# Expert outputs added onto the residual rows in DRAM by indirect DMA, and a last stage of load, norm and store

## The chip, the core and the metric

The kernel runs on one core of a Trainium2 chip. The metric is the device time of one execution in microseconds, as the median of several; less is better.

## What is computed

One decoder block on 2048 tokens of 1024 features, float32. A mixer (gated DeltaNet heads beside dilated window attention) gives the residual rows x2. Then a mixture of experts follows, which the change touches: 32 experts, two for each token, each a SwiGLU with 256 hidden features. At the end stands an RMSNorm of the sum.

```python
xs = xt[buf_tok].reshape(nblk, MOE_BLK, d)
def expert_block(args):
    xb, e = args
    hid = jax.nn.silu(xb @ w_gate[e]) * (xb @ w_up[e])
    return hid @ w_down[e]
ys = lax.map(expert_block, (xs, blk_e)).reshape(P, d)
out = jnp.zeros((T, d), ys.dtype).at[buf_tok].add(ys * buf_w[:, None])
# x = x2 + gate * out ; result = rmsnorm(x, norm_final)
```

`buf_w` is the router's weight of a token for an expert, and `gate` a vector over features that is the same for all tokens.

## The kernel before

Eight stages run one after the other, with a barrier of all engines between them (`PHASES`, L2164). Tensors keep 128 rows on the partitions; the 2048 tokens are 16 tiles.

`mix_out` (L1463) makes the residual rows tile by tile, keeps them in SBUF (`m.x2`, L2210) and stores the normed rows `h` to `m.h_d` (L1657, on ScalarE's queue). Its `residual` on ScalarE (L1652) takes the squares of a tile and then waits for `h`.

`route` (L1684) picks two experts for each token. The tokens of an expert fill whole blocks of 128 slots, up to 96 blocks; here 50 are in use. `m.dest` holds the slot of each token and choice. Thirty-two small indirect DMAs of GpSimd scatter the token numbers into `slot_tok_d` (L1870), which is loaded back as `m.slot_tok`. Unused slots hold token 0.

`experts` (L1876) goes over the blocks in use, with buffers for two blocks (b = 0, 1) and for two experts' weights. Each engine has its own program, in order:

- SP loads the weights of the expert after next: `wgu` (2 MB, L1923) when `gu_done` says that the last block before has been multiplied with it, `wd` (1 MB, L1925) when `y_done` does. The two counters come from the router (`by_expert`). At the end it writes zeros into the unused blocks of `ys_d` (L1935).
- GpSimd gathers the 128 rows of a block from `h_d` (L1949), as soon as the block two earlier has been transposed and the indices are there (L1945 to L1948).
- TensorE, in step t: `turn_x` transposes block t+1 (L1959), `down` makes the output of block t-1 (L1986), then it transposes the hidden tile of t (L2004), and `gate_up` of t+1 follows (L1976).
- ScalarE, in step t: `silu` (L2026), the copy of the transposed rows of t+1 (L2016), the copy of the transposed hidden tile (L2032), and the store of block t-1's output into its own place in `ys_d` (L2020).
- VectorE, in step t: the hidden product (L2058), the indices of block t+2 (L2050), and `take_y` of t-1, the output times `gate` (L2047).

`finish` (L2067) takes the tiles in groups of four. GpSimd gathers the two expert rows of each token from `ys_d` (two indirect DMAs a tile, L2103), ScalarE scales one by its router weight (L2113), VectorE scales and adds the other and adds x2 from SBUF (L2141, L2142), ScalarE takes squares and root (L2116, L2117), VectorE norms (L2146), and ScalarE issues the store (L2120).

A signal's `n(k)` is the semaphore value after k events; `credit` is a start value that every wait adds too.

Of the kernel before, what the change touches and what calls it, by code (L numbers as in the profile page):

```python
# [11 lines left out]
P = 128  # L12
T = 2048
# [1449 lines left out]
def mix_out(nc, m, a):  # L1463
# [5 lines left out]
    with Room(nc, "mo") as R:  # L1469
# [23 lines left out]
        h_out = S("h_out", 2, 16)  # L1493
# [7 lines left out]
        with R.block() as block:  # L1501
# [124 lines left out]
            def _(act):  # L1626
# [54 lines left out]
                for b in range(2):  # L1681
                    act.wait_ge(*h_out[b].n(NT // 2))
                    act.wait_ge(*lg_ready[b].n(NT // 2))
def route(nc, m, a):  # L1684
# [8 lines left out]
    with Room(nc, "ro") as R:  # L1693
# [28 lines left out]
        toki = R.sb("toki", [P, NT], I32)  # L1722
        zero = R.sb("zero", [P, NBLK], I32)
# [15 lines left out]
        with R.block() as block:  # L1739
            @block.sync  # L1740
            def _(sp):

                sp.wait_ge(*zero_set.n(1))
                sp.dma_start(m.slot_tok_d, zero[:, :]).then_inc(*zero_out.inc)
                sp.wait_ge(*tok_all.n(1))
                sp.dma_start(m.slot_tok[:, 0:NBLK], m.slot_tok_d).then_inc(*tok_in.inc)
                sp.wait_ge(*tok_in.n(1))

            @block.vector
            def _(dve):  # L1750
# [11 lines left out]
                V.memset(zero[:, :], 0).then_inc(*zero_set.inc)  # L1762
                link(V.memset(m.slot_tok[:, NBLK:NBLK + 1], 0))
# [46 lines left out]
                link(V.tensor_copy(toki[:, :], m.cst[:, C_TOK:C_TOK + NT]))  # L1810
# [53 lines left out]
            def _(pool):  # L1864
                pool.wait_ge(*pos_ready.n(1))
                pool.wait_ge(*zero_out.n(1))
                flat = m.slot_tok_d.rearrange("p b -> (p b)").unsqueeze(1)
                for t in range(NT):
                    for n in range(2):
                        pool.indirect_dma_start(out=flat, out_offset=bass.IndirectOffsetOnAxis(ap=pos[:, n, t:t + 1].bitcast(U32), axis=0),  # L1870
                                                in_=toki[:, t:t + 1], in_offset=None).then_inc(tok_out, 16)
# [4 lines left out]
def experts(nc, m, a):  # L1876
# [4 lines left out]
    with Room(nc, "ex") as R:  # L1881
        idx = R.sb("idx", [P, 2], I32)
# [12 lines left out]
        zero_set, zero_out, seen_sp = R.sig("zero_set"), R.sig("zero_out", 16), R.plain("seen_sp")  # L1895
        seen_act = R.plain("seen_act")
# [3 lines left out]
        ht_done, ht_ready, y_ready, out = S("ht_done"), S("ht_ready"), S("y_ready"), S("out", 2, 16)  # L1900
# [13 lines left out]
        with R.block() as block:  # L1914
            @block.sync
            def _(sp):
                with sp.Fori(0, NE // 2) as i:
# [12 lines left out]
                pairs = sp.value_load(m.pairs[0:1, 0:1], min_val=1, max_val=NBLK // 2 - 1)  # L1930
                sp.wait_ge(*zero_set.n(1))
                with sp.Fori(0, NBLK // 2 - 1) as i:
                    with sp.If(pairs <= i):
                        for b in range(2):
                            sp.dma_start(one(m.ys_d, 2 * i + (2 + b)), zero[:, :]).then_inc(*zero_out.inc)  # L1935
                unused = sp.value_load(m.pairs[0:1, 1:2], min_val=0, max_val=NBLK // 2 - 1)
                sp.wait_ge(*zero_out.n(unused * 2))
                sp.sem_inc(seen_sp, 1)

            @block.gpsimd  # L1940
            def _(pool):
                rows = m.h_d.rearrange("t p n -> (t p) n")
                for t, b, q, head, tail in blocks(pool):

                    pool.wait_ge(*xt_done[b].n(q))  # L1945
# [4 lines left out]
                                            in_offset=bass.IndirectOffsetOnAxis(ap=idx[:, b:b + 1].bitcast(U32), axis=0)).then_inc(xg_in[b], 16)  # L1950

# [59 lines left out]
            def _(act):  # L2011
# [6 lines left out]
                def store_y(t, b, q):  # L2018
                    act.wait_ge(*y_ready[b].n(q + 1))
                    act.dma_start(one(m.ys_d, t), y[:, b, :]).then_inc(*out[b].inc)  # L2020

                take_x(0, 0, 0)
                for t, b, q, head, tail in blocks(act):
# [12 lines left out]
                for b in range(2):  # L2036
                    act.wait_ge(*out[b].n(q + 1))
                    act.sem_inc(seen_act, 1)

            @block.vector  # L2040
            def _(dve):
                nc.vector.memset(zero[:, :], 0.0).then_inc(*zero_set.inc)

                def take_y(t, b, q):
                    dve.wait_ge(*y_done.n(t + 1))
                    dve.wait_ge(*out[b].n(q))
                    nc.vector.tensor_tensor(y[:, b, :], ps[:, 6:8, :].rearrange("p n w -> p (n w)"), gate, ALU.mult).then_inc(*y_ready[b].inc)  # L2047
# [19 lines left out]
def finish(nc, m, a):  # L2067
# [3 lines left out]
    with Room(nc, "fi") as R:  # L2071
        idx = R.sb("idx", [P, NBUF, 2], I32)
        yg = R.sb("yg", [P, NBUF, 2, D])
# [3 lines left out]
        ss = R.sb("ss", [P, NBUF])  # L2077
        eps = R.sb("eps", [P, 1])
        def S(name, step=1):
            return R.sigs(name, NBUF, step)  # L2080

        gain_in, eps_set = R.sig("gain_in", 16), R.sig("eps_set")
        yg_in, seen = [R.plain(f"yg_in{b}") for b in range(NBUF)], R.plain("seen")
        idx_ready, scaled, sum_ready, sq_ready, o_ready, out = S("idx_ready"), S("scaled"), S("sum_ready"), S("sq_ready"), S("o_ready"), S("out", 16)
        dve_self, act_self = R.plain("dve_self"), R.plain("act_self")
        N = NT // NBUF
        with R.block() as block:
            @block.sync
            def _(sp):
                sp.dma_start(gain[:, :], row_bc(a["norm_final"], D)).then_inc(*gain_in.inc)  # L2090

            @block.gpsimd
            def _(pool):
                rows = m.ys_d.rearrange("t p n -> (t p) n")
                with pool.Fori(0, N) as i:
                    for b in range(NBUF):

                        pool.wait_ge(*sum_ready[b].n(i))
                        pool.sem_inc(seen, 1)
                        pool.wait_ge(*idx_ready[b].n(i + 1))  # L2100
                        pool.sem_inc(seen, 1)
                        for n in range(2):
                            pool.indirect_dma_start(out=yg[:, b, n, :], out_offset=None, in_=rows,  # L2103
                                                    in_offset=bass.IndirectOffsetOnAxis(ap=idx[:, b, n:n + 1].bitcast(U32), axis=0)).then_inc(yg_in[b], 16)

            @block.scalar
            def _(act):
                link = Chain(act, act_self)
                act.wait_ge(*eps_set.n(1))
                with link.loop(N, NBUF) as i:  # L2110
                    for b in range(NBUF):
                        act.wait_ge(yg_in[b], i * 32 + 32)
                        nc.scalar.activation(yg[:, b, 0, :], yg[:, b, 0, :], ACT.Copy, scale=m.gate[:, 0, bass.ds(NBUF * i + b, 1)]).then_inc(*scaled[b].inc)  # L2113
                    for b in range(NBUF):
                        act.wait_ge(*sum_ready[b].n(i + 1))
                        link(nc.scalar.activation(junk[:, :], o[:, b, :], ACT.Square, accum_out=ss[:, b:b + 1]))  # L2116
                        nc.scalar.activation(ss[:, b:b + 1], ss[:, b:b + 1], ACT.Sqrt, bias=eps[:, :], scale=1.0 / D).then_inc(*sq_ready[b].inc)  # L2117
                    for b in range(NBUF):
                        act.wait_ge(*o_ready[b].n(i + 1))
                        act.dma_start(one(m.out, NBUF * i + b), o[:, b, :]).then_inc(*out[b].inc)  # L2120
                for b in range(NBUF):
                    act.wait_ge(*out[b].n(N))

            @block.vector
            def _(dve):
                link = Chain(dve, dve_self)
                V = nc.vector
                V.memset(eps[:, :], EPS).then_inc(*eps_set.inc)
                dve.wait_ge(*gain_in.n(1))

                def take_idx(t, b):
                    V.tensor_copy(idx[:, b, :], m.dest[:, :, bass.ds(t, 1)].rearrange("p n a -> p (n a)")).then_inc(*idx_ready[b].inc)  # L2132

                def tiles(i, ahead):
                    for b in range(NBUF):
                        dve.wait_ge(*scaled[b].n(i + 1))
                        dve.wait_ge(yg_in[b], i * 32 + 32)
                        if ahead:
                            take_idx(NBUF * i + NBUF + b, b)
                        dve.wait_ge(*out[b].n(i))  # L2140
                        link(V.scalar_tensor_tensor(o[:, b, :], yg[:, b, 1, :], m.gate[:, 1, bass.ds(NBUF * i + b, 1)], yg[:, b, 0, :], ALU.mult, ALU.add))  # L2141
                        V.tensor_tensor(o[:, b, :], o[:, b, :], one_tile(m.x2, NBUF * i + b), ALU.add).then_inc(*sum_ready[b].inc)  # L2142
                    for b in range(NBUF):
                        dve.wait_ge(*sq_ready[b].n(i + 1))
                        link(V.reciprocal(ss[:, b:b + 1], ss[:, b:b + 1]))  # L2145
# [114 lines left out]
```

## Time and profile before

| | us |
|---|---|
| median of 3 runs | 2682.29 |
| lowest and highest | 2680.24, 2687.91 |
| the profiled execution, its own time | 2681.78 |
| its span in the trace | 2679.9 |

| engine | busy us | share |
|---|---|---|
| TensorE, matmul | 2272.5 | 85% |
| VectorE | 1104.7 | 41% |
| ScalarE | 805.8 | 30% |
| GpSimd | 329.6 | 12% |

The span goes from the first instruction to the last. PE is TensorE, DVE VectorE, ACT ScalarE, POOL GpSimd, SP SyncE; a q behind the name is that engine's sequencer, which issues DMAs. The DMA line of the page gives the busy share of the 16 DMA engines in tenths, for 40 equal slices of the span, each 67 us. "Landing" is the time from the issue of a DMA to its last arrival.

### The profile page before, as it was taken

To read this page: it belongs to the slowest core of one execution; us is meant where nothing else is said; L and a number is where in the kernel's file an instruction comes from. 1 tells how busy PE (TensorE), PEld (TensorE's weight loads), DVE (VectorE), ACT (ScalarE), POOL (GpSimd) and SP (SyncE) were. 2 spreads that over 40 slices of the span, in tenths; PEclk is the share of its full clock that TensorE was granted. 3 is DMA by queue.
4 is the path that set the end of the run, shared out by engine and by line. 5 is a ranking of instruction groups with operands and counts; after the bars stand their busy time and mean duration, and the time that the engine had idled before them with its cause. 6 is when DMAs were issued, how large, how long until landed. Compare 5 with 4: busy or idle time off the path is not lost. (4 is left out here: it accounts for less than half of the span.)

```text
span 2679.9 us, 31777 instructions
## 1 busy us (share of the span) xinstructions
PE 2272.5 (85%) x9218; PEld 1329.4 (50%) x9219; DVE 1104.7 (41%) x2029; ACT 805.8 (30%) x2123; POOL 329.6 (12%) x314
## 2 busy tenths in 40 slices
PE   3999899999888978949999959999169999999940
PEld 2666444444444458926777735555024444444410
DVE  5444132322346525526788845654501111111127
ACT  1433111111333112216777834442011111111125
POOL 0000000000111014411133400000310000000022
PEclk9999999999999989969999979999579999999975
DMA  8443011112456549723233333331058766579767
GB/s 337 146 135 135 33 55 63 55 63 87 137 176 194 176 130 296 237 97 115 95 88 95 104 110 127 127 127 44 5 186 308 242 229 218 202 265 328 270 249 283
DMA packets 178532, 426.63 MB, mean 159 GB/s; under 512 B 41824, under 2 KB 77920, under 8 KB 162960
## 3 DMA queue, kind: packets, MB, share of 16 engines
q1 hardware_dynamic: 153664, 335.37, 36.9%
q0 software_dynamic: 12832, 43.02, 4.7%
q10 hardware_dynamic: 11952, 47.19, 4.3%
q8 instruction: 45, 0.74, 0.1%
q14 instruction: 39, 0.32, 0.0%
HBM read 304.44 MB, written 121.07 MB: 159 GB/s over the span
## 5 line engine op out<-in xcount | busy, mean ns | idle before, releaser
L627 PE MATMUL ps<-big,pc_w 128*128 128x512 f32 x1280 | 556.8, 596 | 10.1 <-DMA pc_w<-in_w_chan 10.1
L627 PEld LDWEIGHTS ps<-big,pc_w 128*128 128x128 f32 x1280 | 243.3, 191 | 310.5 <-issue 299.5
L1976 PE MATMUL ps<-ex_wgu,ex_xt 128*128 x800 | 359.1, 602 | 24.2 <-DMA ex_wgu<-in_w_gate_up 23.5
L1976 PEld LDWEIGHTS ps<-ex_wgu,ex_xt 128*128 128x128 f32 x800 | 150.3, 193 | 198.9 <-issue 198.9
L310 PE MATMUL ps<-cp_wt,big 128*128 128x344 f32 x768 | 225.5, 454 | 0.0
L1562 PE MATMUL ps<-w_out,mo_yt 128*128 128x512 f32 x512 | 225.0, 598 | 0.0
L1372 PE MATMUL ps<-at_v,at_pt 128*128 128x128 f32 (+1 forms) x1200 | 183.1, 290 | 6.2 <-DMA at_v<-v_d 6.2
L1986 PE MATMUL ps<-ex_wd,ex_hidt 128*128 x400 | 181.8, 598 | 4.3 <-issue 2.9
L310 PEld LDWEIGHTS ps<-cp_wt,big 128*128 128x128 f32 x768 | 145.9, 191 | 76.9 <-issue 4.1
L1434 ACT ACTIVATE at_p<-at_p,at_low 128x256 f32<-128x256 f32 (+1 forms) x384 | 174.0, 456 | 20.1 <-DVE at_low L1401 19.7
L1372 PEld LDWEIGHTS ps<-at_v,at_pt 128*128 128x128 f32 x1200 | 149.1, 191 | 52.8 <-issue 35.7
L2058 DVE TENSOR_TENSOR ex_hid<-ex_sg,ps 128x256 f32<-128x256 f32 x50 | 21.1, 421 | 362.1 <-ACT ex_sg L2026 340.1
L1562 PEld LDWEIGHTS ps<-w_out,mo_yt 128*128 128x128 f32 x512 | 97.2, 192 | 116.5 <-issue 116.5
L1399 DVE SCALAR_TENSOR_TENSOR at_p<-ps,bias 128x512 f32<-128x512 f32 (+1 forms) x192 | 109.3, 569 | 69.9 <-PE ps L1347 69.4
L2047 DVE TENSOR_TENSOR ex_y<-ps,mod 128x1024 f32<-128x1024 f32 x50 | 61.2, 1225 | 174.6 <-PE ps L1986 174.6
L2026 ACT ACTIVATE ex_sg<-ps 128x256 f32<-128x256 f32 x50 | 19.3, 386 | 356.7 <-PE ps L1976 356.7
L1347 PE MATMUL ps<-at_kb,at_qb 64*128 64x256 f32 (+1 forms) x768 | 119.5, 389 | 6.1 <-POOL at_kb L1333 5.1
L1949 POOL DMA_INDIRECT ex_xg<-h_d,ex_idx x50 | 47.3, 945 | 545.9 <-DVE ex_idx L2050 499.2
L1417 ACT COPY at_pt<-ps 128x512 f32<-128x512 f32 (+1 forms) x192 | 93.8, 488 | 66.5 <-PE ps L1357 61.1
L782 DVE TENSOR_SCALAR pc_cv<-pc_pre,pc_wc 128x2048 f32<-128x2048 f32 x12 | 15.4, 1287 | 234.5 <-ACT pc_pre L707 234.5
L1401 DVE TENSOR_REDUCE at_low<-at_p 128x2 f32<-128x512 f32 (+1 forms) x192 | 109.4, 570 | 6.6
L1986 PEld LDWEIGHTS ps<-ex_wd,ex_hidt 128*128 128x128 f32 x400 | 72.7, 192 | 78.2 <-issue 78.2
(289 smaller groups left out, 2866.5 us busy)
## 6 DMA issues: line engine op xcount, KB each, us to landing
ex_wgu<-in_w_gate_up SPq DMA_DIRECT2D x32, 2048.0 KB, 11.1
ex_wd<-in_w_down SPq DMA_DIRECT2D x32, 1024.0 KB, 7.8
ys_d<-ex_y ACTq DMA_DIRECT2D x50, 512.0 KB, 8.0
cp_w<-in_w_ada SPq DMA_DIRECT2D x24, 1024.0 KB, 5.4
ch_d<-pc_cv SPq DMA_DIRECT2D x20, 1024.0 KB, 3.9
at_v<-v_d SPq DMA_DIRECT2D x27, 512.0 KB, 3.9
o_d<-at_o SPq DMA_DIRECT2D x48, 264.0 KB, 2.1
mo_o<-o_d SPq DMA_DIRECT2D x16, 792.0 KB, 6.6
```

The source lines that it names most:

```text
L310: last = nc.tensor.matmul(ps[:, ROW_A + g, 0:THIRD], m.ht[:, k, t * P:(t + 1) * P], wt[:, k, g * THIRD:(g + 1) * THIRD], start=(k == 0), s ...
L627: last = nc.tensor.matmul(ps[:, n % 2, :], w[:, ch % 2, k, :], m.ht[:, k, g * BANK:(g + 1) * BANK], start=(k == 0), stop=(k == KD - 1))
L1347: last = nc.tensor.matmul(ps[:, 2 * (s % 2) + h, lo:2 * P], qb[r, b, s, :], kb[r, b, s, lo:], start=True, stop=True)
L1372: last = nc.tensor.matmul(ps[:, 6 + b, w], pt[:, e, h, k, :], v[:, b, k, w], start=(k == k0), stop=(k == 1))
L1399: nc.vector.scalar_tensor_tensor(p[:, s, :, lo:], ps[:, 2 * e:2 * e + 2, lo:2 * P], DH ** -0.5, m.bias[:, unit[0][1], 2 * s:2 * s + 2, lo: ...
L1401: nc.vector.tensor_reduce(low[:, b, 2 * s:2 * s + 2], p[:, s, :, lo:], AX.X, ALU.max, negate=True).then_inc(*max_ready[e].inc)
L1417: nc.scalar.copy(pt[:, e, :, k:, :], ps[:, 4 + e, :].rearrange("p (h k n) -> p h k n", h=2, k=2)[:, :, k:, :]).then_inc(*pt_ready[e].inc)
L1434: ins = nc.scalar.activation(p[:, s, h, lo:], p[:, s, h, lo:], ACT.Exp, bias=low[:, b, at:at + 1], accum_out=low[:, b, at + AH:at + AH + 1])
L1562: last = nc.tensor.matmul(ps[:, 2 + 2 * b + n, :], yt[:, b, k, :], w[:, k, n * BANK:(n + 1) * BANK], start=(k == 0), stop=(k == KD - 1))
L1976: last = nc.tensor.matmul(ps[:, 2 + b, :], xt[:, b, k, :], wgu[:, bass.ds(half * WGU + k * 2 * DE, 2 * DE)], start=(k == 0), stop=(k == KD ...
L1986: last = nc.tensor.matmul(ps[:, 6 + n, :], hidt[:, b, k, :], wd[:, bass.ds(half * WD + (k * D + n * BANK), BANK)], start=(k == 0), stop=(k ...
L2047: nc.vector.tensor_tensor(y[:, b, :], ps[:, 6:8, :].rearrange("p n w -> p (n w)"), gate, ALU.mult).then_inc(*y_ready[b].inc)
```

## The change

- `mix_out` also stores each tile of x2 to a new DRAM tensor `acc_d`, on ScalarE's queue, before it waits for `h`.
- `route` scatters pairs of the token number and its router weight (8 bytes in place of 4). Unused slots now hold the numbers T to T+127, which are an extra tile of `h_d` and of `acc_d`, and the weight 0.
- `experts` writes zeros into those two extra tiles first, and GpSimd waits for them. `take_y` multiplies by the slot's router weight and by `gate` in one instruction, and copies the row numbers into `to`. GpSimd adds the block's rows onto `acc_d` with an accumulating indirect DMA, one block after the other: each add waits until ScalarE has seen the one before land. ScalarE issues no store. The zeros into unused blocks go.
- `finish` loads a tile of `acc_d` (SP), takes squares and root (ScalarE), norms (VectorE) and stores (SP). There are no gathers, no scaling and no sums in it.

```diff
@@ mix_out, ScalarE, residual
+                    act.dma_start(one(m.acc_d, t), x2(b, q)).then_inc(*x2_out.inc)
                     act.wait_ge(*h_ready[b].n(q + 1))
@@ route
+                for n in range(2):
+                    link(V.tensor_copy(toki[:, n, :, 0], m.cst[:, C_TOK:C_TOK + NT]))
+                    link(V.tensor_copy(toki[:, n, :, 1].bitcast(F32), m.gate[:, n, :]))
@@ experts
+        added = R.sig("added", credit=2)
@@ experts, SP
+                sp.wait_ge(*zero_set.n(1))
+                sp.dma_start(m.h_d[NT], zero[:, :]).then_inc(*zero_out.inc)
+                sp.dma_start(m.acc_d[NT], zero[:, :]).then_inc(*zero_out.inc)
@@ experts, GpSimd
-                for t, b, q, head, tail in blocks(pool):
-
+                sums = m.acc_d.rearrange("t p n -> (t p) n")
+
+                def gather(b, q):
                     pool.wait_ge(*xt_done[b].n(q))
                     pool.sem_inc(seen, 1)
                     pool.wait_ge(*idx_ready[b].n(q + 1))
                     pool.sem_inc(seen, 1)
                     pool.indirect_dma_start(out=xg[:, b, :], out_offset=None, in_=rows,
                                             in_offset=bass.IndirectOffsetOnAxis(ap=idx[:, b:b + 1].bitcast(U32), axis=0)).then_inc(xg_in[b], 16)
+
+                def add_y(s, b, q):
+
+                    pool.wait_ge(*y_ready[b].n(q + 1))
+                    pool.sem_inc(seen, 1)
+                    pool.wait_ge(*added.n(s))
+                    pool.sem_inc(seen, 1)
+                    pool.indirect_dma_start(out=sums, out_offset=bass.IndirectOffsetOnAxis(ap=to[:, b:b + 1].bitcast(U32), axis=0),
+                                            in_=y[:, b, :], in_offset=None, compute_op=ALU.add).then_inc(out[b], 16)
+
+                pool.wait_ge(*zero_out.n(2))
+                gather(0, 0)
+                for t, b, q, head, tail in blocks(pool):
+                    if not tail:
+                        gather(*after(b, q))
+                    if not head:
+                        add_y(t - 1, *before(b, q))
+                add_y(t, 1, q)
@@ experts, ScalarE
                     if not head:
-                        store_y(t - 1, *before(b, q))
-                store_y(t, 1, q)
+                        b1, q1 = before(b, q)
+                        act.wait_ge(out[b1], q1 * 16 + 16)
+                        act.sem_inc(*added.inc)
+                act.wait_ge(out[1], q * 16 + 16)
+                act.sem_inc(*added.inc)
@@ experts, VectorE, take_y
-                    dve.wait_ge(*out[b].n(q))
-                    nc.vector.tensor_tensor(y[:, b, :], ps[:, 6:8, :].rearrange("p n w -> p (n w)"), gate, ALU.mult).then_inc(*y_ready[b].inc)
+                    dve.wait_ge(*added.n(t - 1))
+                    nc.vector.tensor_copy(to[:, b:b + 1], m.slot_tok[:, bass.ds(t, 1), 0])
+                    nc.vector.scalar_tensor_tensor(y[:, b, :], ps[:, 6:8, :].rearrange("p n w -> p (n w)"), m.slot_tok[:, bass.ds(t, 1), 1].bitcast(F32), gate, ALU.mult, ALU.mult).then_inc(*y_ready[b].inc)
@@ finish
+                def load(t):
+                    if t >= NBUF:
+                        sp.wait_ge(*o_ready.n(t - NBUF + 1))
+                    sp.dma_start(x[:, t % NBUF, :], m.acc_d[t]).then_inc(*x_in[t % NBUF].inc)
...
+                for t in range(NT):
+                    sp.wait_ge(*o_ready.n(t + 1))
+                    sp.dma_start(m.out[t], o[:, t % NBUF, :]).then_inc(*out[t % NBUF].inc)
+                    if t + NBUF < NT:
+                        load(t + NBUF)
```

## Rows read from the trace of the kernel before

**Rows 1.** The page: DMA engines' busy share in tenths, 40 slices of the span
```profile
DMA  8443011112456549723233333331058766579767
```

**Rows 2.** TensorE's waits, 1990 to 2582 us: waiter, releaser, total us, times, longest
```profile
PE ps L1976 <- DMA ex_wgu<-in_w_gate_up: 19.3, 12, 2.9
...
PE ps L1959 <- DMA ex_xg<-h_d,ex_idx: 1.8, 2, 1.5
```

**Rows 3.** Timeline of one block: start us, us, engine, line, operation, tiles, count
```profile
2082.66 1.22 DVE L2047 TENSOR_TENSOR ex_y<-ps,mod 128x1024 f32<-128x1024 f32 x1 [3.41 <-PE ps L1986]
2082.68 7.03 PE L1976 MATMUL ps<-ex_wgu,ex_xt 128*128 x16
...
2089.55 1.04 PE L1959 MATMUL ps<-cst,ex_xg 128*128 128x128 f32 x8
...
2090.67 0.14 DVE L2050 COPY ex_idx<-slot_tok 128x1 int32 x1
...
2091.62 0.94 POOL L1949 DMA_INDIRECT ex_xg<-h_d,ex_idx  x1 [10.62 <-DVE ex_idx L2050]
...
2094.06 1.23 DVE L2047 TENSOR_TENSOR ex_y<-ps,mod 128x1024 f32<-128x1024 f32 x1 [3.24 <-PE ps L1986]
```

**Rows 4.** Tiles ex_xg, ex_y, ex_wd: count, ns min/median/max, first and last start; landing
```profile
L1949 POOL DMA_INDIRECT ex_xg<-h_d,ex_idx x50: 943/944/977, 1959.5 to 2545.0; - x50
...
DMA to landing us min/median/max: 4.2/5.0/10.9
...
L2047 DVE TENSOR_TENSOR ex_y<-ps,mod x50: 1223/1225/1226, 1993.7 to 2579.5; 128x1024 f32<-128x1024 f32 x50
...
L1925 SPq DMA_DIRECT2D ex_wd<-in_w_down x32: 332/333/343, 1961.4 to 2524.8; - x32
...
DMA to landing us min/median/max: 5.4/7.8/16.4
```

**Rows 5.** Timeline of SP's queue, 2060 to 2085 us: weight loads as issued
```profile
2060.00 0.33 SPq L1925 DMA_DIRECT2D ex_wd<-in_w_down  x1
2067.09 0.33 SPq L1923 DMA_DIRECT2D ex_wgu<-in_w_gate_up  x1
2082.80 0.33 SPq L1925 DMA_DIRECT2D ex_wd<-in_w_down  x1
2084.99 0.34 SPq L1923 DMA_DIRECT2D ex_wgu<-in_w_gate_up  x1
```

**Rows 6.** Windows: us, busy (x) PE PEld DVE ACT POOL; then PEclk, DMA share, GB/s
```profile
2010.00:2015.00 5.00, 5.00 (x19) 2.60 (x18) 0.48 (x2) 1.40 (x2) 0.90 (x1) 1.00 1.04 427
...
2020.00:2030.00 10.00, 10.00 (x27) 4.78 (x26) 0.48 (x2) 1.17 (x2) 0.00 (x0) 0.83 0.80 320
...
2450.00:2500.00 50.00, 44.76 (x132) 21.20 (x130) 6.37 (x12) 7.08 (x12) 3.78 (x4) 1.00 0.88 323
...
2600.00:2680.00 80.00, 0.00 (x0) 0.00 (x0) 62.03 (x76) 47.32 (x70) 25.85 (x25) 0.50 0.77 286
```

**Rows 7.** Timeline of the first block of the expert stage
```profile
1970.26 9.88 PE L1976 MATMUL ps<-ex_wgu,ex_xt 128*128 x16 [4.20 <-DMA ex_wgu<-in_w_gate_up]
```

**Rows 8.** Timeline of the last stage: its first DMA, first copy and last instruction
```profile
2586.05 0.36 SPq L2090 DMA_DIRECT2D fi_gain<-in_norm_final  x1
2589.77 0.38 DVE L2132 COPY fi_idx<-dest 128x2 int32<-128x2 int32 x4 [4.73 <-DMA fi_gain<-in_norm_final]
...
2674.66 1.29 DVE L2146 SCALAR_TENSOR_TENSOR fi_o<-fi_o,fi_ss,fi_gain 128x1024 f32<-128x1024 f32 x1
```

**Rows 9.** Tile fi_o of the last stage: scaled sums and squares
```profile
L2141 DVE SCALAR_TENSOR_TENSOR fi_o<-fi_yg,gate x16: 1276/1278/1286, 2600.3 to 2667.8; 128x1024 f32<-128x1024 f32 x16
...
L2116 ACT ACTIVATE fi_junk<-fi_o x16: 1039/1040/1057, 2607.3 to 2670.4; 128x1024 f32<-128x1024 f32 x16
```

**Rows 10.** Groups of the mixer's output stage, ScalarE: busy, mean ns, idle before, releaser
```profile
L1633 ACT ACT_TABLE_LOAD x13 | 16.7, 1283 | 44.4 <-DVE mo_h L1608 44.4
```

**Rows 11.** Tile ro_toki of the route stage: the scatters
```profile
L1870 POOL DMA_INDIRECT slot_tok_d<-ro_toki,ro_pos x32: 963/967/2230, 1910.5 to 1951.8; - x32
```

More of the change, by code:

```diff
@@ L1492, in mix_out @@
         x2_ready, xsq_ready, h_ready = S("x2_ready"), S("xsq_ready"), S("h_ready")
-        h_out = S("h_out", 2, 16)
+        h_out, x2_out = S("h_out", 2, 16), R.sig("x2_out", 16)
         def x2(b, q):
@@ L1682, in _ @@
                     act.wait_ge(*h_out[b].n(NT // 2))
+                    act.wait_ge(*x2_out.n(NT))
                     act.wait_ge(*lg_ready[b].n(NT // 2))
@@ L1721, in route @@
         sq2 = R.sb("sq2", [P, NE, NE])
-        toki = R.sb("toki", [P, NT], I32)
-        zero = R.sb("zero", [P, NBLK], I32)
+        toki = R.sb("toki", [P, 2, NT, 2], I32)
+        blank = R.sb("blank", [P, NBLK, 2], I32)
         ps = m.ps
@@ L1760, in first_of @@
                     link(V.tensor_tensor(one_hot, iota(n), over(idx[:, :], n), ALU.is_equal))
-                V.memset(zero[:, :], 0).then_inc(*zero_set.inc)
-                link(V.memset(m.slot_tok[:, NBLK:NBLK + 1], 0))
+                link(V.tensor_scalar(blank[:, :, 0], m.cst[:, C_TOK:C_TOK + 1].to_broadcast([P, NBLK]), float(T), None, ALU.add))
+                V.memset(blank[:, :, 1], 0).then_inc(*zero_set.inc)
+                dve.wait_ge(*zero_set.n(1))
+                link(V.tensor_copy(m.slot_tok[:, NBLK, :], blank[:, 0, :]))
                 link(V.tensor_reduce(gm[:, :], gl, AX.X, ALU.max))
@@ L1866, in _ @@
                 pool.wait_ge(*zero_out.n(1))
-                flat = m.slot_tok_d.rearrange("p b -> (p b)").unsqueeze(1)
+                flat = m.slot_tok_d.rearrange("p b x -> (p b) x")
                 for t in range(NT):
@@ L1881, in experts @@
     with Room(nc, "ex") as R:
-        idx = R.sb("idx", [P, 2], I32)
+        idx, to = R.sb("idx", [P, 2], I32), R.sb("to", [P, 2], I32)
+        by = R.sb("by", [P, 2])
         xg = R.sb("xg", [P, 2, D])
@@ L1899, in experts @@
         xt_done, xt_ready, sg_ready, hid_ready = S("xt_done"), S("xt_ready"), S("sg_ready"), S("hid_ready")
-        ht_done, ht_ready, y_ready, out = S("ht_done"), S("ht_ready"), S("y_ready"), S("out", 2, 16)
+        ht_done, ht_ready, y_ready, out = S("ht_done"), S("ht_ready"), S("y_ready"), [R.plain("out0"), R.plain("out1")]
+        added = R.sig("added", credit=2)
         gate = m.mod[:, 5 * D:6 * D]
@@ L1928, in _ @@
                     sp.wait_ge(*wd_in[b].n(NE // 2))
[L1930 to L1938, printed above, removed]
             @block.gpsimd
@@ L2016, in take_x @@
                     nc.scalar.copy(xt[:, b, :, :].rearrange("p k n -> p (k n)"), ps[:, 0:2, :].rearrange("p k n -> p (k n)")).then_inc(*xt_ready[b].inc)
-                def store_y(t, b, q):
-                    act.wait_ge(*y_ready[b].n(q + 1))
-                    act.dma_start(one(m.ys_d, t), y[:, b, :]).then_inc(*out[b].inc)
                 take_x(0, 0, 0)
@@ L2033, in _ @@
                     if not head:
-                        store_y(t - 1, *before(b, q))
-                store_y(t, 1, q)
-                for b in range(2):
-                    act.wait_ge(*out[b].n(q + 1))
-                    act.sem_inc(seen_act, 1)
+                        b1, q1 = before(b, q)
[3 more added lines that the diff above has]
+                act.sem_inc(*added.inc)
             @block.vector
@@ L2071, in finish @@
     with Room(nc, "fi") as R:
-        idx = R.sb("idx", [P, NBUF, 2], I32)
-        yg = R.sb("yg", [P, NBUF, 2, D])
+        x = R.sb("x", [P, NBUF, D])
         gain = R.sb("gain", [P, D])
@@ L2076, in finish @@
         junk = R.sb("junk", [P, D])
-        ss = R.sb("ss", [P, NBUF])
+        ss = R.sb("ss", [P, NT])
         eps = R.sb("eps", [P, 1])
-        def S(name, step=1):
-            return R.sigs(name, NBUF, step)
         gain_in, eps_set = R.sig("gain_in", 16), R.sig("eps_set")
-        yg_in, seen = [R.plain(f"yg_in{b}") for b in range(NBUF)], R.plain("seen")
-        idx_ready, scaled, sum_ready, sq_ready, o_ready, out = S("idx_ready"), S("scaled"), S("sum_ready"), S("sq_ready"), S("o_ready"), S("out", 16)
+        x_in, out = R.sigs("x_in", NBUF, 16), R.sigs("out", NBUF, 16)
+        sq_ready, o_ready = R.sig("sq_ready"), R.sig("o_ready")
         dve_self, act_self = R.plain("dve_self"), R.plain("act_self")
-        N = NT // NBUF
         with R.block() as block:
@@ L2089, in _ @@
             def _(sp):
-                sp.dma_start(gain[:, :], row_bc(a["norm_final"], D)).then_inc(*gain_in.inc)
[L2092 to L2104, printed above, removed]
+                def load(t):
+                    if t >= NBUF:
+                        sp.wait_ge(*o_ready.n(t - NBUF + 1))
+                    sp.dma_start(x[:, t % NBUF, :], m.acc_d[t]).then_inc(*x_in[t % NBUF].inc)
+                load(0)
+                load(1)
+                sp.dma_start(gain[:, :], row_bc(a["norm_final"], D)).then_inc(*gain_in.inc)
+                for t in range(2, NBUF):
+                    load(t)
+                for t in range(NT):
[3 more added lines that the diff above has]
+                        load(t + NBUF)
+                for b in range(NBUF):
+                    sp.wait_ge(*out[b].n(NT // NBUF))
             @block.scalar
@@ L2109, in _ @@
                 act.wait_ge(*eps_set.n(1))
[L2110 to L2122, printed above, removed]
+                for t in range(NT):
+                    b = t % NBUF
+                    act.wait_ge(*x_in[b].n(t // NBUF + 1))
+                    link(nc.scalar.activation(junk[:, :], x[:, b, :], ACT.Square, accum_out=ss[:, t:t + 1]))
+                    nc.scalar.activation(ss[:, t:t + 1], ss[:, t:t + 1], ACT.Sqrt, bias=eps[:, :], scale=1.0 / D).then_inc(*sq_ready.inc)
             @block.vector
@@ L2126, in _ @@
                 link = Chain(dve, dve_self)
-                V = nc.vector
-                V.memset(eps[:, :], EPS).then_inc(*eps_set.inc)
+                nc.vector.memset(eps[:, :], EPS).then_inc(*eps_set.inc)
                 dve.wait_ge(*gain_in.n(1))
[L2131 to L2145, printed above, removed]
-                        V.scalar_tensor_tensor(o[:, b, :], o[:, b, :], ss[:, b:b + 1], gain[:, :], ALU.mult, ALU.mult).then_inc(*o_ready[b].inc)
-                for b in range(NBUF):
-                    take_idx(b, b)
-                with link.loop(N - 1, 2 * NBUF) as i:
-                    tiles(i, True)
-                tiles(N - 1, False)
+                for t in range(NT):
+                    b = t % NBUF
+                    dve.wait_ge(*sq_ready.n(t + 1))
+                    link(nc.vector.reciprocal(ss[:, t:t + 1], ss[:, t:t + 1]))
+                    dve.wait_ge(*x_in[b].n(t // NBUF + 1))
+                    dve.wait_ge(*out[b].n(t // NBUF))
+                    nc.vector.scalar_tensor_tensor(o[:, b, :], x[:, b, :], ss[:, t:t + 1], gain[:, :], ALU.mult, ALU.mult).then_inc(*o_ready.inc)
 class Shared:
@@ L2199, in block_kernel @@
         m.o_d = dram("o_d", [NB, NT, P, AW + 2 * AH])
-        m.h_d = dram("h_d", [NT, P, D])
-        m.slot_tok_d = dram("slot_tok_d", [P, NBLK], I32)
-        m.ys_d = dram("ys_d", [NBLK, P, D])
+        m.h_d, m.acc_d = dram("h_d", [NT + 1, P, D]), dram("acc_d", [NT + 1, P, D])
+        m.slot_tok_d = dram("slot_tok_d", [P, NBLK, 2], I32)
         m.ch_d = dram("ch_d", [m.NCH, P, T])
```

14 lines of the change are left out of this document (6 added, 8 removed).

## The prediction

> **What bounds the kernel now.** I read the page's slices first. In the last quarter the DMA digits stand at 5 to 9 [rows 1]: the expert stage, where 3 MB of weights per expert stream past TensorE. The wait list of TensorE for that stage is nearly empty: 19.3 us in 12 waits for `ex_wgu`, 1.8 us for gathered rows [rows 2]. So TensorE bounds the stage, with DMA close behind. The timeline of one block gives the cycle [rows 3]. Call T the moment at which VectorE takes block t-1's output (2082.66). Then `gate_up` of t+1 runs 7.03 us, the transposes of `turn_x` for t+2 start at T+6.9, `down` of t follows, and its output is taken at 2094.06. That is a block of 11.4 us, of which 4.5 us lie between the start of `turn_x` and the next T. Over the stage 49 blocks take from 1993.7 to 2579.5, mean 11.95 [rows 4]. The rest over 11.4 is mostly weights that come late.
>
> What matters is when the gather for t+2 starts. Today GpSimd issues it 0.8 us after the index copy, which is before T: in these rows the copy is at 2090.67, the gather at 2091.62 and the T of that round at 2094.06, so 2.4 us before T [rows 3]. It has some 9.4 us until `turn_x`, and lands in 4.2 us at best, 5.0 in the median, 10.9 at worst [rows 4]. All of that is hidden.
>
> **The change, part by part.**
>
> *Expert stage, GpSimd's order.* This is the term that decides. GpSimd's program becomes: gather(t+1), add(t-1), gather(t+2), add(t), and so on, and each add waits for `y_ready`. GpSimd works in order, so gather(t+2) stands behind the wait of add(t-1). Step by step from T: VectorE copies the row indices (0.14, as the index copy) and runs the scaled product, priced at 1.28 as its kind costs in the last stage [rows 9], so `y_ready` is at T+1.4. GpSimd reacts after 0.8 [rows 3], so the add starts at T+2.2. An indirect DMA holds GpSimd 0.94 us [rows 4], and with the gap the 32 scatters of the route stage come every 1.33 us [rows 11], so gather(t+2) is issued at T+3.5. It must have landed by T+6.9: 3.4 us, where the shortest of 50 gathers took 4.2. TensorE must wait in every block, even if the add itself is free: T+7.7.
>
> *What the add adds.* No row shows an accumulating transfer. From below it is one copy of 512 KB, 1.2 us at the 427 GB/s that the DMA engines reached in one stretch [rows 6], and since it is issued 1.3 us ahead it then delays the gather by nothing. From above nothing in the trace limits it. I take two copies' time, 2.5 us, because it reads the product and the old row and writes one: the gather lands 1.2 us later, at T+8.9. For the high end I take four copies, 4.9 us, T+11.4. The Trainium skill (Collectives: The Full Stack, "The bandwidth ceiling") says that a reduce in the DMA engines runs at about half the rate of a copy because it reads two sources; no run here shows it, and it would leave the sum as it is.
>
> A block without other load is then 8.9 + 4.5 = 13.4 us.
>
> *Blocks under weight load.* SP issues `wd` of a coming expert 0.14 us after T, and in 19 of the 30 cases `wgu` follows 1.9 to 2.2 us later (in the others 7 us or more) [rows 5]. There 1 MB and 2 MB (2.5 and 4.9 us) stand before or beside the add (2.5) and the gather (1.2) on the same engines. The fixed part of a transfer is 2.9 to 3.0 us: 4.2 less 1.2 for the gather, 5.4 less 2.5 for `wd` [rows 4]. The gather, last in its queue, lands at 0.14 + 2.9 + 2.5 + 4.9 + 2.5 + 1.2 = T+14.1, so such a block is 18.6 us. Today some of these blocks are late already: they hold the 19.3 us of waits for `ex_wgu` [rows 2], and the DMA engines move 323 GB/s over 50 us [rows 6].
>
> Stage: 19 x 18.6 + 30 x 13.4 = 755 us against 586 now: **+170**.
>
> *TensorE's clock.* In one stretch of 10 us TensorE was granted 0.83 of its full clock, so 1.2 GHz for part of it, right after it had stood waiting, and the first `gate_up` after a long pause took 9.88 us instead of 7.03 [rows 6, 7]. In the 19 loaded blocks TensorE would idle 7 us before `turn_x`, and the work after it lies in the loop. I take 1.5 us each, half of that 2.85: **+28**; from below nothing, from above 1.5 us in all 49, +73.
>
> *ScalarE's new wait.* It no longer issues the store but waits until the add has landed before it takes `silu` of t+1. Behind it are `sg`, `hid` and then `turn_x`'s copy. The add always lands before the gather that is queued behind it, and `sg` and `hid` (under 1 us) fit into the 4.5 us after that gather. Cost nothing, as long as the gather is the later one. The wait of each add for the one before is covered too: the add lands some 5.5 us after its issue, 11 under load, and the next is due a block later.
>
> *The product on VectorE* costs 1.28 instead of 1.22: counted in T+1.4.
>
> *Last stage.* From its first DMA at 2586 to the end of the span at 2680 it now takes 94 us; the last instruction starts at 2674.66 [rows 8]. It moves 25 MB (32 gathers and 16 stores of 512 KB); the new one moves 16.8 MB (16 loads, 16 stores). At 427 GB/s that is 39 us, at the stage's 286 [rows 6] it is 59; I take 350, 48 us. ScalarE (1.04 for the square, some 0.5 for the rest) and VectorE (1.29 plus a reciprocal) need some 1.5 us a tile [rows 8, 9], less than the 3 us of DMA, and four buffers hold it: a load of 3.7 us (as the gain's, 2586.05 to 2589.77), the two engines and the issues make 8 us for four tiles. First landing at 2589.8 and last tile plus store add about 8: 56 us. **-38** (-48 to -27).
>
> *Entry.* The weights are issued behind two stores of zeros (1 MB, 2.5 us), and the first gather, issued at 1959.5 so far [rows 4], waits for both to land, some 4 us. The first `gate_up` at 1970.26 waits for weights [rows 7]: **+3** (0 to 6). *Exit:* instead of two stores the last two adds, one after the other, each 0.8 us later through GpSimd and with 1.2 us more of data: **+5** with the landing between them (2 to 10). The zeros into unused blocks stood behind the last weight load, beside TensorE's work, and free nothing on the path.
>
> *Mixer and route.* 16 more stores of 512 KB on ScalarE's queue, 0.33 us to issue each, as SP's loads [rows 4]: ScalarE has 44.4 us of idle time right behind that place [rows 10], and DMA is a third busy there [rows 1]. If that cover went, 5 us. The scatters carry 8 bytes instead of 4; GpSimd's pitch sets them. Three more small copies: **+1**.
>
> **Sum:** 170 + 28 - 38 + 3 + 5 + 1 = +169 on the profiled execution's 2681.8 us (span 2679.9), 0.5 us under the median of 2682.3: **2850 us**. Low end: gather at T+7.7 in quiet blocks (12.2) and 16.0 in loaded ones gives +84, no clock loss, the last stage at -48: about 2723. High end: the add at four copies gives 15.9 and 21.1, +292, the clock +73, the last stage -27, +12 at the ends: about 3030.
>
> **Rivals.** (1) *The gather hides after all: faster.* It needs the gather to land within 3.4 us of its issue, with the add not in its way. Then only the last stage and the ends count, 2682 - 38 + 8 = 2652. Against it: 4.2 is the least of 50 [rows 4]. For it: an unloaded transfer of this size could in principle be near that edge, and GpSimd could react quicker. The Trainium skill (DMA: Bandwidth & Descriptors, "Anatomy of one DMA") fits a GpSimd DMA as 2.0 us plus bytes over 436 GB/s; that makes 3.2 us for this gather and would give this very case; the trace disagrees, with 4.2 at least. Chance 0.06. The point from which it decides: at less than 0.7 us of wait a block the last stage pays for it all.
> (2) *The add is slow and everything follows its landing.* Each block is then 2.2 + D + 1.2 + 4.5, D the add's time to landing. D = 15 gives 22.9 us a block, +536, about 3190 with the rest. Nothing in the trace speaks for or against it but the rate of a copy. Chance 0.13.
> (3) *Gains and stalls cancel:* the same, between 2674 and 2690, chance 0.02. The forecast with its bounds has 0.79.
>
> **Numbers.** The chance of faster by over 0.3% (about what a measurement of this kernel tells from no change) is rival 1, 0.06; within 0.3% 0.02; slower 0.92. The range 2735 to 3010 leaves out rivals 1 to 3 for the most part and the thin ends of the bounds.
>
> **What the profile after would show.** TensorE's wait for `ex_xg` before `turn_x` rises from 1.8 us to 100 to 250 us, with 45 or more waits, and its wait for `ex_wgu` shrinks. The gather starts about 3.5 us after VectorE begins `ex_y`, right behind the add on GpSimd, and lands 5 to 11 us later. ScalarE's `sg` waits for a DMA instead of TensorE. The last stage ends some 56 us after its start. The forecast is wrong if TensorE's wait is small (the gather was quicker), if the add's landing takes over 12 us, or if the wait of `turn_x` is for ScalarE or GpSimd and not for the gather.

## The result, and the profile after

The changed kernel takes 2986.11 us (median of 4 runs, 2982.82 to 2995.98) against 2682.22: a ratio of 1.1135, 95% interval 1.1104 to 1.1167. That is 304 us slower. The forecast was 2850, with a range of 2735 to 3010: the time lies inside the range, 24 us under its upper end, and the forecast itself was 136 us short.

The spans of the two profiled executions, cut at the first and last product `ex_y` and at the first DMA of the last stage, say where the time went:

| stretch, us | before | after | difference | forecast |
|---|---|---|---|---|
| up to the first `ex_y` | 1993.7 | 2002.1 | +8.4 | +4 |
| first to last `ex_y`, 49 blocks | 585.8 | 915.6 | +329.8 | +198 |
| last `ex_y` to the last stage's first DMA | 6.5 | 15.1 | +8.6 | +5 |
| last stage, to the end of the span | 93.9 | 48.2 | -45.7 | -38 |
| span | 2679.9 | 2981.0 | +301.1 | +169 |

TensorE's waits in the expert stage, 1990 to 2918 us, which answer to [rows 2] (waiter, releaser, total us, times, longest):

```profile
PE ps L1978 <- DMA ex_xg<-h_d,ex_idx: 265.1, 47, 9.1
```

It was 1.8 us in 2 waits, and is now 265.1 in 47, at the line of `turn_x`. No wait for weights is left. The timeline of one quiet block, that is one without a load of `wgu` right behind T, to be read against [rows 3]:

```profile
2258.63 7.03 PE L1995 MATMUL ps<-ex_wgu,ex_xt 128*128 x16
2258.72 0.15 DVE L2062 COPY ex_to<-slot_tok 128x1 int32 x1 [13.59 <-PE ps L2005]
...
2258.85 1.28 DVE L2063 SCALAR_TENSOR_TENSOR ex_y<-ps,slot_tok,mod 128x1024 f32<-128x1024 f32 x1
2261.14 1.59 POOL L1959 DMA_INDIRECT acc_d<-ex_y,ex_to  x1 [20.57 <-DVE ex_y L2063]
2263.04 0.97 POOL L1950 DMA_INDIRECT ex_xg<-h_d,ex_idx  x1 [0.30 <-issue]
2268.28 0.38 ACT L2041 ACTIVATE ex_sg<-ps 128x256 f32<-128x256 f32 x1 [9.07 <-DMA acc_d<-ex_y,ex_to]
...
2269.57 1.09 PE L1978 MATMUL ps<-cst,ex_xg 128*128 128x128 f32 x8 [3.91 <-DMA ex_xg<-h_d,ex_idx]
2270.50 5.30 PE L2005 MATMUL ps<-ex_wd,ex_hidt 128*128 x8
...
2276.03 0.15 DVE L2062 COPY ex_to<-slot_tok 128x1 int32 x1 [6.77 <-PE ps L2005]
```

T, at which VectorE turns to block t-1's output, is 2258.72. GpSimd's lines show the two indirect DMAs back to back, the add at T+2.4 and the gather behind it at T+4.3. TensorE has finished `gate_up` at 2265.66 and stands 3.91 us. Then `down`, 3.60 us before, takes 5.30. The block is 17.3 us where it was 11.4. Of the 49 blocks 27 are quiet like this one (15.0 to 18.1 us, median 16.9), 20 take 20.3 to 23.4, and the last two are short.

The tiles `ex_xg` and `ex_y` of the same kernel (count, ns min/median/max, first and last start; below each the time to landing), for [rows 4]:

```profile
L1950 POOL DMA_INDIRECT ex_xg<-h_d,ex_idx x50: 938/975/978, 1965.3 to 2885.6; - x50
...
DMA to landing us min/median/max: 5.6/6.7/13.2
...
L2063 DVE SCALAR_TENSOR_TENSOR ex_y<-ps,slot_tok,mod x50: 1283/1284/1285, 2002.1 to 2917.7; 128x1024 f32<-128x1024 f32 x50
L1959 POOL DMA_INDIRECT acc_d<-ex_y,ex_to x50: 1549/1592/1634, 2004.4 to 2920.4; - x50
...
DMA to landing us min/median/max: 6.0/6.4/12.1
```

An accumulating indirect DMA holds GpSimd for 1.59 us, where a gather holds it for 0.98, and lands after 6.4 us in the median. ScalarE is idle for 501.4 us in front of `silu` until adds have landed, which looks like a cause. It was a rival in the experiments.

The windows show the clock (columns as in [rows 6]):

```profile
2250.00:2300.00 50.00, 40.60 (x102) 19.46 (x102) 5.21 (x10) 4.92 (x8) 7.70 (x6) 0.86 0.41 111
2700.00:2800.00 100.00, 59.84 (x154) 30.30 (x153) 8.08 (x18) 7.70 (x14) 11.76 (x10) 0.81 0.61 202
```

TensorE's granted clock is 0.86 and 0.81 on average, so part of nearly every block runs at 1.2 GHz. It was 1.00 over the 50 us from 2450 before [rows 6]. The DMA engines move 111 and 202 GB/s, less than the 323 before, so on average they are not the bound; within a loaded block the gather still waits behind the weights, as the experiments show.

The page's group of `down`, first before and then after, says what the clock costs there:

```profile
L1986 PE MATMUL ps<-ex_wd,ex_hidt 128*128 x400 | 181.8, 598 | 4.3 <-issue 2.9
...
L2005 PE MATMUL ps<-ex_wd,ex_hidt 128*128 x400 | 237.6, 750 | 4.1 <-issue 4.1
```

The same 400 matmuls take 56 us more. Over the stage (1994 to 2580 us before, 2002 to 2918 after) TensorE is busy 559 us before and 645 after, for the same matmuls: 86 of the 330 us are what half clock costs, and the other 244 are waiting.

### The profile page after: what moved, and what is told of

It is laid out like the page before. It is cut to its first block and busy times, and to the rows that moved or that the text cites. A ratio compares the mean times of both kernels' runs of the same rounds, so it can differ in the third digit from the quotient of the medians.

```text
span 2981.0 us, 31595 instructions
## 1 busy us (share of the span) xinstructions
PE 2360.1 (79%) x9218; PEld 1375.4 (46%) x9219; DVE 1075.2 (36%) x2035; ACT 779.4 (26%) x2100; POOL 377.2 (13%) x332
## 5 line engine op out<-in xcount | busy, mean ns | idle before, releaser
L1978 PE MATMUL ps<-cst,ex_xg 128*128 128x128 f32 x400 | 84.5, 381 | 339.6 <-DMA ex_xg<-h_d,ex_idx 339.6
L1978 PEld LDWEIGHTS ps<-cst,ex_xg 128*128 128x128 f32 x400 | 66.4, 195 | 381.0 <-DMA ex_xg<-h_d,ex_idx 233.8
L2005 PE MATMUL ps<-ex_wd,ex_hidt 128*128 x400 | 237.6, 750 | 4.1 <-issue 4.1
L1959 POOL DMA_INDIRECT acc_d<-ex_y,ex_to x50 | 79.6, 1592 | 791.3 <-DVE ex_y L2063 402.6
L2041 ACT ACTIVATE ex_sg<-ps 128x256 f32<-128x256 f32 x50 | 19.2, 383 | 529.0 <-DMA acc_d<-ex_y,ex_to 501.4
L2005 PEld LDWEIGHTS ps<-ex_wd,ex_hidt 128*128 128x128 f32 x400 | 98.1, 259 | 112.4 <-issue 112.4
L2062 DVE COPY ex_to<-slot_tok 128x1 int32 x50 | 7.7, 154 | 336.5 <-PE ps L2005 336.5
```

The source lines that it names most:

```text
L1959: pool.indirect_dma_start(out=sums, out_offset=bass.IndirectOffsetOnAxis(ap=to[:, b:b + 1].bitcast(U32), axis=0), in_=y[:, b, :], in_offse ...
L1978: last = nc.tensor.transpose(ps[:, k // 4, (k % 4) * P:(k % 4 + 1) * P], xg[:, b, k * P:(k + 1) * P], m.ident)
L2005: last = nc.tensor.matmul(ps[:, 6 + n, :], hidt[:, b, k, :], wd[:, bass.ds(half * WD + (k * D + n * BANK), BANK)], start=(k == 0), stop=(k ...
```

## The experiments

The theory: gather(t+2) stands behind the wait and the issue of add(t-1) in GpSimd's program, and TensorE waits for it. The rivals: the accumulating transfer itself, and ScalarE's wait for its landing. Ratios are against the kernel before, run on the same chip (2677.26 us for the first four runs, 2681.10 for the last three, 2682.22 for the change itself), so a difference of two medians from different groups can be off by some 5 us. Each run's expert stage is its first to last `ex_y`.

### The gather first

```diff
                 gather(0, 0)
+                gather(1, 0)
                 for t, b, q, head, tail in blocks(pool):
                     if not tail:
-                        gather(*after(b, q))
+                        gather(b, q + 1)
                     if not head:
                         add_y(t - 1, *before(b, q))
                 add_y(t, 1, q)
+                pool.wait_ge(xg_in[0], q * 16 + 32)
```

It gathers one block more than is used.

> The changed kernel, GpSimd issuing the gather of block t+2 before the add of block t-1. Theory (the gather stands behind the wait and issue of the add, and TensorE waits for it): the gather is early again, TensorE's wait for ex_xg before turn_x falls from some 400 us to under 40, quiet blocks go from 16.9 us back to 11.4, blocks under weight load to 12 to 14.5, limited by ScalarE's wait for the landing. Whole kernel 2660 us, 2640 to 2710. Rival A (the add itself is slow, or ScalarE's wait for it sets the pace): the order hardly matters, over 2900.

Measured: 2707.56 us, ratio 1.0115 (1.0078 to 1.0153); the stage takes 641.1 us, 275 less than with the add first. The wait for `ex_xg` is gone. What TensorE waits for now, in the stage's wait lists of TensorE and of all engines:

```profile
PE ps L2025 <- DVE ex_hid L2076: 47.4, 15, 5.2
```

```profile
ACT ex_sg L2043 <- DMA acc_d<-ex_y,ex_to: 464.3, 44, 15.0
...
PEld ps L2025 <- DVE ex_hid L2076: 63.0, 20, 6.0
```

It waits for the hidden tile in 20 blocks. In 15 of them its matmul waits too, 47.4 us in all. The 63.0 us of the weight loads cover the same waits, so the two must not be added (the 110 us in the expectation of `both` are such a sum). The hidden tile waits for `silu`, which waits for the landing of the add. So putting the gather first takes away five sixths of the stage's loss, and behind it the rival's wait appears as the next bound. The time is 48 us over the value I had named, though inside its range.

### ScalarE does not wait

The order stays that of the change; GpSimd itself waits for the add before and then raises `added`, for VectorE. (The loop is peeled by two blocks, so that no wait has the value zero.)

```diff
-                    pool.wait_ge(*added.n(s))
-                    pool.sem_inc(seen, 1)
+                    if not is_tile(s, 0):
+                        b1, q1 = before(b, q)
+                        pool.wait_ge(out[b1], q1 * 16 + 16)
+                        pool.sem_inc(*added.inc)
...
-                    if not head:
-                        b1, q1 = before(b, q)
-                        act.wait_ge(out[b1], q1 * 16 + 16)
-                        act.sem_inc(*added.inc)
```

> The changed kernel with its order kept, but ScalarE no longer waits for the landing of an add; GpSimd waits for it itself before the next add. Theory (the gather's place is the cause, ScalarE's wait lies under it): the same time within 15 us of 2986. Rival A (ScalarE's wait in front of silu, 501 us of idle time in the profile, sets the pace): falls by over 150 us.

Measured: 2987.32 us, 1.1147 (1.1094 to 1.1199), stage 914.6 against 915.6. The 501 us of ScalarE's waiting cost nothing in this order. In the profile after, `silu` could start 0.8 us or more before `turn_x` in every block (1.3 us in the one shown), and TensorE needs the hidden tile only behind `turn_x` and `down`. The rival is out as the cause of the loss.

### No accumulate

```diff
-                                            in_=y[:, b, :], in_offset=None, compute_op=ALU.add).then_inc(out[b], 16)
+                                            in_=y[:, b, :], in_offset=None).then_inc(out[b], 16)
```

The rows are written over and not added, so this kernel leaves the sums out.

> The changed kernel with the accumulate left out of the indirect DMA: the rows are written instead of added, so the sums are left out of the computation. Theory: GpSimd needs 0.95 instead of 1.59 us to issue it and the transfer takes one copy's time instead of two, so the gather behind it lands 1.8 us earlier: 49 x 1.8 = 90 us less, 2895, 2860 to 2930; blocks still 14.5 us and more, since the order is kept. Rival B (accumulating is the cost, not the order): back to some 2700.

Measured: 2846.66 us, 1.0630 (1.0595 to 1.0664), stage 785.6, so rival B is out: with the accumulate gone and the order kept, 200 of the stage's 330 us stay. Its tile `ex_y`:

```profile
L1959 POOL DMA_INDIRECT acc_d<-ex_y,ex_to x50: 962/986/997, 1997.7 to 2783.2; - x50
...
DMA to landing us min/median/max: 3.3/3.8/11.1
```

So the accumulate costs 0.6 us more on GpSimd (1.59 against 0.99), and 2.7 us more from issue to landing at best (6.0 against 3.3), of which 2.1 lie behind GpSimd's part. The fall of 139 us is larger than expected, and the time is 13 us under my range. A quiet block shows why:

```profile
2241.50 0.15 DVE L2062 COPY ex_to<-slot_tok 128x1 int32 x1 [7.37 <-PE ps L2005]
...
2245.22 0.96 POOL L1950 DMA_INDIRECT ex_xg<-h_d,ex_idx  x1 [0.30 <-issue]
...
2249.82 1.09 PE L1978 MATMUL ps<-cst,ex_xg 128*128 128x128 f32 x8 [1.38 <-DMA ex_xg<-h_d,ex_idx]
2250.75 3.60 PE L2005 MATMUL ps<-ex_wd,ex_hidt 128*128 x8
...
2254.59 0.15 DVE L2062 COPY ex_to<-slot_tok 128x1 int32 x1 [5.03 <-PE ps L2005]
```

TensorE waits only 1.38 us, and `down` is at 3.60 us again: full clock. The block is 13.1 us. With the accumulate it waits 3.9 us and pays 1.7 us more at half clock (6.5 us from `turn_x` to the next T, against 4.8 here).

### TensorE kept busy while it waits

```diff
-                def turn_x(b, q):
+                def turn_x(b, q, fill=True):
+                    if fill:
+                        for k in range(4):
+                            nc.tensor.matmul(ps[:, 5, :], m.ident, m.cst[:, 0:BANK], start=True, stop=True)
                     pe.wait_ge(xg_in[b], q * 16 + 16)
```

> The changed kernel with four unused matmuls 128x512 (some 3.5 us) on TensorE before its wait for the gathered rows, into a free PSUM bank. Theory (after the wait TensorE runs at half clock, so turn_x and down take 6.5 us instead of 4.5): with its idle time filled the quiet blocks go from 16.9 to about 15, the loaded ones less: 60 to 98 us less, 2905, 2880 to 2930. Rival C (the slow down has another cause, or the clock does not matter for the loop): the same or slower by up to 10 us.

Measured: 2944.13 us, 1.0983 (1.0946 to 1.1020), 42 us less (35 in the profiled executions); expected were 60 to 98. In the timeline of a quiet block:

```profile
2244.55 0.15 DVE L2065 COPY ex_to<-slot_tok 128x1 int32 x1 [5.51 <-PE ps L2008]
...
2251.33 3.60 PE L1976 MATMUL ps<-cst 128*128 128x512 f32 x8
...
2254.95 1.09 PE L1981 MATMUL ps<-cst,ex_xg 128*128 128x128 f32 x8
2255.88 3.60 PE L2008 MATMUL ps<-ex_wd,ex_hidt 128*128 x8
...
2259.72 0.15 DVE L2065 COPY ex_to<-slot_tok 128x1 int32 x1 [4.90 <-PE ps L2008]
```

From `turn_x` to the next T it takes 4.8 us, not 6.5, and the block 15.2, as expected. The clock is shown for the quiet blocks: added work made the kernel faster. Over the stage the granted clock rises from 0.86 to 0.94. The loaded blocks, 22 of them now, stayed at 20.5 to 24.1 us. The fill was half as long as their wait, and the row of another stretch says that their clock still fell:

```profile
2700.00:2750.00 50.00, 37.44 (x95) 18.66 (x96) 4.28 (x10) 4.93 (x8) 5.14 (x4) 0.88 0.55 183
```

### Both cures

The edits of the first two experiments together.

> Gather first and no wait on ScalarE for the landing of an add (GpSimd waits for it before the next add). In the run with the gather first alone, silu of t+1 started only when the add had landed, 9.6 us after T and later, and TensorE waited 110 us for the hidden tile. Theory (with the gather out of the way ScalarE's wait is the next bound): that wait goes, blocks 11.4 us quiet and 12.5 to 13.5 under load, 40 to 60 us less than with the gather first: 2655, 2640 to 2680, so faster than the kernel before. Rival D (the added DMA traffic sets the pace of the loaded blocks by itself): no more than 15 us less, about 2695.

Measured: 2655.66 us, 0.9907 (0.9891 to 0.9924): 0.9% faster than the kernel before, with the whole interval under 1, and 11% faster than the change as it was made. The stage takes 589.4 us, 3.6 more than before. TensorE's waits in it:

```profile
PE ps L2012 <- DMA ex_wgu<-in_w_gate_up: 21.6, 8, 3.2
```

That is [rows 2] again, 19.3 us in 12 waits. The accumulating DMAs, with their extra reads, run beside the weights at a cost to the stage of no more than those 3.6 us. Rival D allowed 15 us less than with the gather first alone; it is 52, so it is out. Under the heaviest load the blocks alternate between some 16 and 11.5 us: the eight from 2422 us take 13.8 on average, against 13.0 for the eight from 2421 us in the kernel before.

### The zeros earlier

On top of both cures, the two stores of zeros move into the route stage, where ScalarE, idle there, makes their tile.

```diff
@@ route, SP
+                sp.wait_ge(*pad_set.n(1))
+                sp.dma_start(m.h_d[NT], padz[:, :]).then_inc(*pad_out.inc)
+                sp.dma_start(m.acc_d[NT], padz[:, :]).then_inc(*pad_out.inc)
@@ experts, SP
-                sp.wait_ge(*zero_set.n(1))
-                sp.dma_start(m.h_d[NT], zero[:, :]).then_inc(*zero_out.inc)
-                sp.dma_start(m.acc_d[NT], zero[:, :]).then_inc(*zero_out.inc)
@@ experts, GpSimd
-                pool.wait_ge(*zero_out.n(2))
```

> The same, with the two stores of zeros moved into the route stage, where the DMA engines are idle, so that neither the first weights nor the first gather wait for them. Theory (the first block's 8 us delay, of which 1.5 come from the route stage, is their doing): 5 us less than the run before it, 2 to 7. Rival: no difference.

Measured: 2646.45 us, 0.9868 (0.9851 to 0.9885), 9 us under the run before it, 2 over my upper value; the intervals of the two ratios do not overlap. This is the best version, 35 us under the kernel before. The first `ex_y` is at 1994.7 instead of 1997.2 and the stage 2.4 us shorter in the profiled executions; the rest I can't place from one profile each. So the zeros were 2.5 of the 8.4 us by which the change delayed the first `ex_y`; 4.9 had gone with both cures (2002.1 to 1997.2).

### The order alone, in the kernel before

```diff
                     pool.sem_inc(seen, 1)
+                    if not is_tile(t, 0):
+                        b1, q1 = before(b, q)
+                        pool.wait_ge(*y_ready[b1].n(q1))
+                        pool.sem_inc(seen, 1)
                     pool.wait_ge(*idx_ready[b].n(q + 1))
```

> The kernel before, whose GpSimd now waits for the output of block t-1 before it gathers t+2, and nothing else changed: the order of the change without any add. Theory: the gather is issued at T+2.0 and lands at T+6.2 to T+7 in quiet blocks, which costs next to nothing, and some 6 us too late in the 19 under weight load: 60 to 130 us more, 2770, 2720 to 2820. Rival A (the order is harmless, only the add costs): within 15 us of before.

Measured: 2842.47 us, 1.0597 (1.0579 to 1.0615): 161 us more, without any add, so rival A is out. Most quiet blocks take 11.4 to 13.8 us (one takes 16.7), in many of them next to nothing more, as forecast. The 19 loaded ones take 19.8 to 20.7, so that the time is 22 us over my upper value. One of them:

```profile
2234.31 1.23 DVE L2051 TENSOR_TENSOR ex_y<-ps,mod 128x1024 f32<-128x1024 f32 x1 [3.24 <-PE ps L1990]
...
2234.43 0.33 SPq L1925 DMA_DIRECT2D ex_wd<-in_w_down  x1
...
2236.34 0.33 SPq L1923 DMA_DIRECT2D ex_wgu<-in_w_gate_up  x1
2236.50 0.95 POOL L1953 DMA_INDIRECT ex_xg<-h_d,ex_idx  x1 [10.45 <-DVE ex_y L2051]
...
2247.51 1.97 PE L1963 MATMUL ps<-cst,ex_xg 128*128 128x128 f32 x8 [6.15 <-DMA ex_xg<-h_d,ex_idx]
2249.27 5.14 PE L1990 MATMUL ps<-ex_wd,ex_hidt 128*128 x8
...
2254.45 1.23 DVE L2051 TENSOR_TENSOR ex_y<-ps,mod 128x1024 f32<-128x1024 f32 x1 [12.15 <-PE ps L1990]
```

The gather is issued 0.16 us behind the 2 MB of `wgu` and lands 11 us later (T+13.2; in the quiet blocks it is there by T+9.3 but for one), and `turn_x` and `down` then run at half clock, 6.9 us instead of 4.5. That is the collision that the early gather avoided.

## Why the prediction was right, and where its sizes were off

**Right: the place of the loss.** The gather behind the add, with TensorE's wait before `turn_x` as the bound, is shown in three ways: the order put back takes 275 of the 330 us away, the order alone brings 161 us into the kernel before, and the wait has moved to `ex_xg` (265.1 us in 47 waits; I had said 100 to 250 in 45 or more). The shares overlap and can't be added up: with the order kept, leaving out the accumulate takes 130 us of the same 330. That ScalarE's wait lies under the gather is shown too. The condition that I set for it, "as long as the gather is the later one", mattered: with the gather first, that same wait costs 52 us (641.1 against 589.4), on which the prediction had put no price.

**How near it was.** In the stage I forecast 170 us of waiting and 28 for the clock; measured are 244 and 86. The total stayed in the range because the range's high end had the add at four copies and a clock loss of 1.5 us in every block, blocks of 17.4 and 22.6 us, near the 16.9 and 22.0 measured. That the forecast of 2850 equals the 2847 of `plain_scatter`, whose add costs little more than a copy, is no merit: that kernel has the clock loss in its loaded blocks and few others. In the low end, the loaded blocks of 16.0 us leave the add out altogether; with one copy, as in the quiet ones, they are 17.3 us and the low end some 25 us higher.

**Mis-sized: the quiet block,** 13.4 forecast, some 16.9 measured. By the terms of the sum, on the block shown (17.3):

| term, us | forecast | measured |
|---|---|---|
| T to the add's issue | 2.2 | 2.4 |
| add's issue to the gather's issue | 1.3 | 1.9 |
| gather's issue to `turn_x` | 5.4 | 6.5 |
| `turn_x` to the next T | 4.5 | 6.5 |

The 27 quiet blocks make 93 of the 132 us by which the stage was over its forecast. Half of the miss in the block shown is the last row, and 1.7 of its 2.0 us are *TensorE's clock* (at full clock that stretch takes 4.8 behind a wait). I charged it in the 19 loaded blocks alone, 28 us. The 3.1 to 4.6 us of waiting in each quiet block brought it about as well: in 24 of the 27, some 40 us in all. The fill, which took 1.7 us off a quiet block, shows it. The second and third rows are the accumulate, bounded from the gather's rows: 1.59 us on GpSimd where I took 0.94, and 2.1 us more behind it than for a plain scatter where I allowed 1.3 over one copy. The rule of the Trainium skill (Collectives: The Full Stack, "The bandwidth ceiling"), two reads and so half the rate, gives no more than I took. If all of the 2.1 us is transfer, 1.2 us for the copy and 2.1 more, it goes at little over a third of a copy's rate; that is an estimate, since no run parts a longer transfer from a longer fixed part.

**Mis-sized: the loaded block,** 18.6 plus 1.5 forecast, 20.3 to 23.4 measured in the 20 blocks over 20 us, 22.0 on average. The landing was nearly right, T+14.1 to 15.9 (median 15.1) against T+14.1, but part of that is luck. Without any add the loaded blocks of `late_gather` have it at T+12.9 to 14.0, where my terms without the add's 2.5 us give T+11.6: the weights in front cost more than I took, and the add less. The rest is again the clock: 7.1 us on average from `turn_x` to the next T, 2.6 over the 4.5 where I took 1.5. One of the 20 blocks had its `wgu` load issued 2.7 us behind the gather and not in front of it, and the gather landed at T+15.9 all the same; the model of a queue does not cover that, and no run settles it.

**The ends.** The first gather came at 1965.3, 1.8 us later than forecast, and then took 9.5 us to land beside the weights, so that the first `gate_up` waited for the rows and not for the weights: +8.4 where I had 4. The last two adds cost 8.6, not 5. The last stage gave 46 us, more than the 38: its 16.8 MB in 48.2 us are 348 GB/s with its beginning and end, the rate I took, and the 8 us that I had added for those were not needed.

**The rival that did not come.** The gather within 3.4 us: the shortest was 5.6 behind an accumulating add and 4.1 ahead of it (in `both`), so the trace's 4.2 was the number to trust and not the 3.2 that the Trainium skill's fit gives (DMA: Bandwidth & Descriptors, "Anatomy of one DMA"). The plain scatter's shortest, 3.3, is near that fit, the gather's is not.

**The signs of being wrong.** Of those the prediction named, one came to the letter: the longest landing of an add took 12.1 us, where I had said over 12. The median is 6.4, and the wait of `turn_x` was for the gather.

## What to carry to other kernels

An operation that waits for late data must not be put in front of an early prefetch in the program of one engine: list what stands behind each new wait, and compute when it will be issued and what it will collide with. An idle time of 500 us on an engine off the path proves nothing until the bound in front of it is gone. Then it can be the next bound, so cures have to be tried together. Count the clock for every wait of TensorE that recurs in a loop, not for the long ones alone.

## What the runs showed that I had not expected

- An indirect DMA with an add occupies GpSimd for 1.59 us against 0.99 without, for the same 128 rows.
- Waits of 3.1 to 4.6 us in each block brought half clock in 24 of 27 quiet blocks (`down` at 5.3 us instead of 3.6 in the one shown). With waits of 1.3 to 2.3 us, in `plain_scatter`, it fell in 2 of 28. Four unused matmuls in the wait brought the whole kernel down by 42 us.
- The extra DRAM reads of the accumulate hardly show once the gather is first and ScalarE no longer waits: the stage is 589.4 us against 585.8.
